# Hybrid decoder block on one core: a conv chunk goes first, vector steps follow a hand-written table, GpSimd makes four low halves

## What is computed

```
h = rms_norm(x);  proj = h @ w_in          # ca, cg, q, k, v, iq, ik, iw, z, xbc, dt
conv: u = ca * sigmoid(cg); u = causal depthwise conv of 31 taps
      u = silu(layer_norm(u))
att:  scores of 4 indexer heads -> top 128 keys of each query; softmax attention on them, 8 heads
ssm:  conv of 4 taps and silu on xbc; chunked state-space scan (4 chunks of 128); gate silu(z), rms_norm
x = x + concat([conv, att, ssm]) @ w_out
f = causal conv of 3 taps on rms_norm(x) @ w_up;  x = x + (silu(fg) * fa) @ w_down
```

## Time and profile before

| | us |
|---|---|
| median of 3 runs | 768.38 (765.89 to 770.06) |
| the profiled execution: its own time | 770.06 |
| its span, first to last instruction | 768.3 |
| slot 0 begins | 19.2 |
| slot 12 begins | 69.96 |
| slot 64 begins | 277.56 |
| slot 76 begins | 333.73 |
| the FFN begins | 403.4 |

### The profile page before, as it was taken

How to read it: one execution, slowest core, us unless ns; L and a number is a source line. 1 busy time by engine, 2 the same in 40 slices (tenths; PEclk the granted TensorE clock), 3 DMA queues, 4 the chain that set the end, 5 groups by cost and what they waited for, 6 DMA issues and landing times.

```text
span 768.3 us, 9446 instructions
## 1 busy us (share of the span) xinstructions
PE 729.4 (95%) x3430; PEld 580.7 (76%) x3430; DVE 476.2 (62%) x731; ACT 331.5 (43%) x498; POOL 98.9 (13%) x79
## 2 busy tenths in 40 slices
PE   3999988799999989999969999999999999999998
PEld 2767876676666668888848888888888888888886
DVE  5357899977999957666673656565656665212222
ACT  6245464678546664722443344434443434110110
POOL 2000576642000003333020000000000000000000
PEclk9999999999999999999988999999999999999999
DMA  8541312311111142032221323333243322333302
GB/s 263 150 153 56 110 55 56 110 56 56 55 55 55 56 165 93 23 106 55 82 55 55 110 72 91 109 109 87 77 109 109 98 72 103 110 109 110 104 6 110
DMA packets 78047, 69.46 MB, mean 90 GB/s; under 512 B 5815, under 2 KB 64535, under 8 KB 78015
## 3 DMA queue, kind: packets, MB, share of 16 engines
q1 hardware_dynamic: 77871, 68.51, 28.9%
q10 hardware_dynamic: 144, 0.52, 0.2%
HBM read 66.91 MB, written 2.12 MB: 90 GB/s over the span
## 4 chain that ended last, share of the span: by engine, by line
PE 71%; DVE 12%; ACT 6%; issue 5%; POOL 4%; DMA 1%; SPq 0%; DVEq 0%; POOLq 0%; ACTq 0%
PE bank L1442 62%; DVE u_acc L565 3%; POOL stats L724 2%; DVE w_lo L575 2%; POOL u_acc L744 2%; PE bank L1448 2%; PE bank L1462 2%; ACT w_hi L813 1%; DVE xbcT L1249 1%; DMA x_in<-in_x 1%; PE bank L1684 1%; PE bank L1658 1%; DVE prob L1228 1%; PE bank L1632 1%; ACT prob L928 1%
## 5 line engine op out<-in xcount | busy, mean ns | idle before, releaser
L1442 PE MATMUL bank<-h_hi,w_hi 128*128 128x512 f32 x480 | 192.1, 400 | 1.8 <-DVE h_lo L1080 1.8
L1442 PE MATMUL bank<-h_lo,w_hi 128*128 128x512 f32 x480 | 188.5, 393 | 0.0
L1442 PE MATMUL bank<-h_hi,w_lo 128*128 128x512 f32 x480 | 188.4, 393 | 0.0
L575 DVE TENSOR_TENSOR w_lo<-w_raw,w_hi 128x2048 fp32r<-128x2048 f32 x34 | 79.8, 2348 | 80.7 <-ACT w_hi L813 80.7
L1442 PEld LDWEIGHTS bank<-h_hi,w_hi 128*128 128x128 f32 x480 | 91.2, 190 | 29.3 <-issue 10.6
L1442 PEld LDWEIGHTS bank<-h_hi,w_lo 128*128 128x128 f32 x480 | 91.0, 190 | 19.7
L1442 PEld LDWEIGHTS bank<-h_lo,w_hi 128*128 128x128 f32 x480 | 91.3, 190 | 18.0
L1403 DVE SCALAR_TENSOR_TENSOR f<-bank,prm,f 128x511 f32<-128x511 f32 x88 | 65.8, 747 | 58.1 <-ACT f L1049 51.8
L813 ACT ACTIVATE w_hi<-w_raw 128x2048 fp32r<-128x2048 f32 x34 | 64.9, 1910 | 80.9 <-PE bank L1442 80.3
L1049 ACT ACTIVATE f<-bank,prm 128x512 f32<-128x512 f32 x44 | 33.8, 769 | 102.2 <-PE bank L1442 102.2
L1442 PE MATMUL bank<-w_hi,g_hi 128*128 128x512 f32 x176 | 68.5, 389 | 0.0
(11 more groups left out here) (225 smaller groups left out, 1022.7 us busy)
## 6 DMA issues: line engine op xcount, KB each, us to landing
w_raw<-in_w_up SPq DMA_DIRECT2D x44, 512.0 KB, 4.7
w_raw<-in_w_in SPq DMA_DIRECT2D x34, 512.0 KB, 4.7
w_raw<-in_w_down SPq DMA_DIRECT2D x22, 512.0 KB, 4.4
w_raw<-in_w_out SPq DMA_DIRECT2D x12, 512.0 KB, 4.2
x_in<-in_x SPq DMA_DIRECT2D x4, 512.0 KB, 6.7
tbias<-distance_table SPq DMA_DIRECT2D x1, 2048.0 KB, 8.2
x<-in_x SPq DMA_DIRECT2D x4, 512.0 KB, 6.5
out_x<-y_out SPq DMA_DIRECT2D x8, 256.0 KB, 2.0
```

The source lines that it names most:

```text
L575: eng.tensor_tensor(wlo[:, slot, cols], wraw[:, slot, cols], whi[:, slot, cols].bitcast(F32), ALU.subtract).then_inc(ready, 1)
L1442: ins = pe.matmul(o, a, b, start=first and i == 0 and q == 0, stop=last and i == n - 1 and q == 2)
```

## The change

The order of the plan changes, two step kinds change their ring, and four low halves change their engine. Conv 0 becomes the first chunk and the indexer's the second. `TOP_SLOTS` and `DW_SLOTS` go; the table `FILL` gives for each slot a string, each letter of which takes the next step of a stream: 1, 2, 3 are the top-k steps of a block (with its `sel` at the end), a, c, d are the taps of tiles 0, 2 and 3. Tile 1 is now POOL's, its taps spread from slot 15 to 60 (before: tile 0, 15 to 44). The scores of the indexer move from slots 5, 6, 8 to slots 8 to 11. `ln` moves from slots 66, 67 to 70, 71 and `lnT` from 70, 71 to 73, 74, all in the ring acc. The four `xt` steps stand in slots 65 and 66, two each, where all stood in 65. POOL makes the whole low half of chunks 6, 8, 9 and 10 (before: `POOL_LO` is empty, DVE makes all); who needs one of them waits for POOL's semaphore.

```diff
-CHUNKS = [("iq", 0), ("conv", 0), ("conv", 1)]
+CHUNKS = [("conv", 0), ("iq", 0), ("conv", 1)]
...
-TOP_SLOTS = {1: (9, 36), 2: (9, 42), 3: (9, 48)}
-DW_SLOTS = [(15, 44), (14, 50), (42, 63), (46, 65)]
-LN_SLOTS = (66, 66, 67, 67)
-LNT_SLOTS = (70, 70, 71, 71)
+FILL = {6: "aa", 7: "aaa", 8: "aaa", 10: "1121", 11: "1212", 12: "31213", 14: "2131", 
+        15: "21321", 16: "32112", 18: "31", 19: "23", 20: "121", 21: "3123", 22: "121a", 
+        23: "32131", 24: "2a1321", 25: "32", 26: "1a", 27: "23", 28: "112", 29: "3a1", 
+        30: "23121", 31: "a312", 32: "312a132", 33: "132a23", 34: "23a", 35: "232", 36: "a323", 
+        37: "2a32", 38: "32a33", 39: "a3a3", 40: "3a3a", 42: "cccc", 43: "cccca", 44: "ccac", 
+        46: "dddd", 47: "d", 48: "dddc", 50: "dca", 51: "d", 52: "cdca", 54: "dcd", 55: "c", 
+        56: "dacdd", 58: "cad", 59: "cd", 60: "cdac", 62: "dcda", 63: "cdcd", 64: "dcdc", 
+        65: "dc", 66: "dcdcd", 67: "cdd"}
+POOL_SLOTS = (15, 60)
+LN_SLOTS = (70, 70, 71, 71)
+LNT_SLOTS = (73, 73, 74, 74)
-DW_POOL = 0
+DW_POOL = 1
-POOL_COLS = 640
-POOL_LO = []
+POOL_LO = [6, 8, 9, 10]
...
-    put(3, ("ev", "iq", 0), ("ev", "iq", 1), ("small",), ("ev", "ik", 0))
+    put(3, ("ev", "cg", 0), ("ev", "ca", 0), ("small",), ("ev", "ik", 0))
-    for n, b in ((5, 1), (6, 2), (8, 3)):
-        put(n, *[("idx", b, h) for h in range(NIH)])
+    for n, b, hs in ((8, 1, (0, 1, 2, 3)), (9, 2, (0, 1, 2, 3)), (10, 3, (0, 1)), (11, 3, (2, 3))):
+        put(n, *[("idx", b, h) for h in hs])
...
-        fill[(n if j else at[("conv", 1)]) + 5].append(("glu", j))
+        fill[n + 5].append(("glu", j))
+    spread([("dw", DW_POOL, i) for i in range(CONV_K)], *POOL_SLOTS)
+    spread([("dwp", DW_POOL, i) for i in range(1, CONV_K)], POOL_SLOTS[0] - 1, POOL_SLOTS[1] - 1)
+    for n, letters in FILL.items():
+        fill[n] += [next(streams[v]) for v in letters]
     for t in range(NT):
-        put(LN_SLOTS[t], ("ln", t))
+        fill[LN_SLOTS[t]].append(("ln", t))
         front[LN_SLOTS[t] + 1].append(("lnn", t))
     for j in range(4):
-        put(LNT_SLOTS[j], ("lnT", j))
+        fill[LNT_SLOTS[j]].append(("lnT", j))
-    put(s0 + 1, *[("xt", t) for t in range(NT)])
+    for t in range(NT):
+        put(s0 + 1 + t // 2, ("xt", t))
...
+        elif k in ("ln", "lnT"):
+            group(*s)
...
+        def low(eng, c, ready):
+            eng.wait_ge(w_hi_ready, c + 1)
+            slot = c % NSLOT
+            eng.tensor_tensor(wlo[:, slot, :], wraw[:, slot, :], whi[:, slot, :].bitcast(F32),
+                              ALU.subtract).then_inc(ready, 1)
+        def dve_los(c):
+            return c + 1 - sum(p <= c for p in POOL_LO)
+        def wait_low(eng, c):
+            if c in POOL_LO:
+                eng.wait_ge(pool_lo_ready, POOL_LO.index(c) + 1)
+            else:
+                eng.wait_ge(w_lo_ready, dve_los(c))
```

More of the change, by code:

```diff
@@ L124, in make_plan @@
         fill[4 * c - 3].append(("lo", c))
+    streams = {str(b): iter([(k, b, r) for r in range(TOPK // 8) for k in ("topmax", "topmark")]
+                            + [("sel", b)]) for b in (1, 2, 3)}
+    for j in range(4):
+        streams["abcd"[j]] = iter([("dw", j, i) for i in range(CONV_K)])
     def spread(steps, a, b):
@@ L135, in make_plan @@
     put(2, ("prm",))
-    put(3, ("ev", "iq", 0), ("ev", "iq", 1), ("small",), ("ev", "ik", 0))
+    put(3, ("ev", "cg", 0), ("ev", "ca", 0), ("small",), ("ev", "ik", 0))
     put(4, ("iwT",), ("dt", 0))
-    put(6, ("dt", 1))
-    put(8, ("dt", 2))
-    for n, b in ((5, 1), (6, 2), (8, 3)):
-        put(n, *[("idx", b, h) for h in range(NIH)])
-    for b in (1, 2, 3):
-        spread([(k, b, r) for r in range(TOPK // 8) for k in ("topmax", "topmark")], *TOP_SLOTS[b])
-        fill[TOP_SLOTS[b][1]].append(("sel", b))
+    put(5, ("dt", 1))
+    put(6, ("ev", "iq", 0), ("dt", 2))
+    put(8, ("ev", "iq", 1))
+    for n, b, hs in ((8, 1, (0, 1, 2, 3)), (9, 2, (0, 1, 2, 3)), (10, 3, (0, 1)), (11, 3, (2, 3))):
+        put(n, *[("idx", b, h) for h in hs])
     put(1, ("gtab",))
@@ L175, in make_plan @@
         n = at[("conv", j)]
-        put(n + 2, ("ev", "cg", j))
-        put(n + 4, ("ev", "ca", j))
-        fill[(n if j else at[("conv", 1)]) + 5].append(("glu", j))
[L179 to L182, removed]
+        if j:
+            put(n + 2, ("ev", "cg", j))
+            put(n + 4, ("ev", "ca", j))
+        fill[n + 5].append(("glu", j))
[3 more added lines that the diff above has]
+        fill[n] += [next(streams[v]) for v in letters]
     for t in range(NT):
-        put(LN_SLOTS[t], ("ln", t))
+        fill[LN_SLOTS[t]].append(("ln", t))
         front[LN_SLOTS[t] + 1].append(("lnn", t))
     for j in range(4):
-        put(LNT_SLOTS[j], ("lnT", j))
+        fill[LNT_SLOTS[j]].append(("lnT", j))
     for m in range(8):
@@ L251, in make_groups @@
         k = s[0]
-        if k in ("prm", "idx", "ln", "lnT", "qkT", "cs", "iwT", "yT"):
+        if k in ("prm", "idx", "qkT", "cs", "iwT", "yT"):
             aux.append(s)
+        elif k in ("ln", "lnT"):
+            group(*s)
         elif k == "score":
@@ L746, in _ @@
                 elif k == "lo" and s[1] in POOL_LO:
-                    part_lo(pool, s[1], pool_lo_ready)
+                    low(pool, s[1], pool_lo_ready)
                 elif k == "seg":
@@ L1145, in _ @@
                         op1=ALU.mult).then_inc(dta_ready, 1)
-                elif k == "lo":
-                    part_lo(dve, s[1], w_lo_ready)
+                elif k == "lo" and s[1] not in POOL_LO:
+                    low(dve, s[1], w_lo_ready)
                 elif k == "glu":
@@ L1424, in _ @@
             for c in range(DN0 + 1, len(CHUNKS)):
-                part_lo(dve, c, w_lo_ready)
+                low(dve, c, w_lo_ready)
             for t in range(NT):
@@ L1523, in _ @@
                             pe.wait_ge(hi_evac, HIGH.index(("hT", NT - 1, 1)) + 1)
+                            claim(pe, "cg", 0)
+                            claim(pe, "ca", 0)
                             first_pass(whi, hhi, True, False)
@@ L1740, in _ @@
                 c = DN0 + j
[L1741 removed]
+                wait_low(pe, c)
                 pe.wait_ge(glo_ready, 2 * j + 3)
```

28 lines of the change are left out of this document (8 added, 20 removed).

## The result

The changed kernel takes **779.15 us** (median, 777.46 to 780.66) against 768.34 for the kernel before on the same chip: ratio 1.0145 [1.0114, 1.0177], slower by 10.8 us. The forecast was 766.7 with a range of 758 to 776, so the result lies outside it, on the side of rival (c). The profiled execution took 777.46 us, its span is 775.7 (before 768.3). One execution of a later version (the split of `xt` alone) took 1463 us with every matmul of 512 columns at 677 ns; it is left out of that version's comparison by time, and the version ran once more for a profile.

The account below looks back on a forecast made before the run. PE, busy 95% of the span, was taken as the bound, with DVE pacing it in the middle stages. Terms -0.5 - 5.1 + 0 - 4.5 + 6.7 + 1.7 = -1.7 us against the median 768.38 gave 766.7, range 758 to 776.

Parts of the forecast that it names:

- rival (c): Slower: waits at slots 71, 74, 76 each bring a clock drop, low halves stop DVE 4.1 us; about 776; 0.30 with (d).
- its own lateness is hidden: POOL's low halves: done 5 us after the high half ends, while PE needs them 11 us after the slot began.
- The price of a lock: DVE stopped by each POOL low half: 2.5 us taken, bounds 0.6 and 4.1, top-k steps covering part.
- the strict rule: DVE and GpSimd's shared pair is locked for the whole instruction, so each POOL low half costs DVE 4.1 us.
- slots 12 to 35: DVE relieved but still setting the pace at 76.9 us against PE's 69.9; counted as -5.1 us.
- The late layer norm: Slots 70 to 76: new PE waits of +3.0, +3.2 and +4.8 us at slots 71, 74 and 76, sum +11.0.
- they lie close together, so I take one: Slots 70 to 76: three stalls of 3 to 5 us counted as one clock drop, +1.7 us, ends 0 and +5.
- 47 to 63: Slots where DVE loses 14 of 41 taps and PE becomes the bound: -4.5 us of 5.1 to win.
- 64 to 69: Slots where splitting xt covers ACT's copy: -2.4, clock drop -1.7, start -0.2, sum -4.3 us; -5.9 with moved transposes.
- Rival (a): POOL's low halves stop DVE under 1 us each, first stage PE-bound: total -10.7 us, 757.7; chance 0.26.
- (b): Late layer norm hidden, DVE entering slot 70 with less behind it: half of 11.0 goes, -7.2, about 761; chance 0.10.
- (d): ACT, behind POOL in its scaling steps, holds attention's exps in slots 38 to 58: 771; counted into the slower case, 0.30.

Follow-up runs that it names:

- the first version: The kernel before with only the late layer norm (ln in slots 70 and 71, lnT in 73 and 74, both in the ring acc): 785.45 us, ratio 1.0257.

## Why the prediction was wrong

**Where it failed first: "its own lateness is hidden."** The forecast had the high half end 3 us into slot 4c - 4 and POOL done 5 us later. In the trace ACT's high half of chunk 8 ended at 128.33, 9.6 us into its slot, because ACT stood for POOL's taps (and POOL, before that, for DVE's sums of squares), and POOL then did a power and a tap first. PE waited 7.9 us at chunks 6 and 8. Put right by itself the lateness gave back 3.4 us up to the logit, but only 0.9 at slot 47, since the locks stayed. I had read ACT's waits for POOL's taps and used them against the scalings only, not against the `hi` step behind them in the same queue. The operation was mis-sized too: 4.8 us in the middle, 4.1 forecast.

**The price of a lock.** The value taken was 2.5 us per low half, between 0.6 and 4.1. Measured: 3.6, 4.0 and 3.8, and next to nothing for the fourth. The choice rested on top-k steps standing in between; but POOL started while DVE was just ahead of a norm step or a mask, and only 0.9, 0.8 and 0.2 us of the three lengths were covered by steps that ran on. Three low halves stand ahead of the logit, so this is 3.9 us more of DVE's time. For these three the upper end was right, and the strict rule with it; the fourth had the cover that was hoped for. With the low halves back on DVE the same stretch takes 78.8 us, where the forecast's own sum without locks is 63.9 + 6.9 + 5.5 = 76.3: the count of DVE's work was off by 2.5 us, the two terms for POOL by more: together they were to cost 0.6 us net (7.5 for locks less 6.9 of work), and cost 6.4. Of the 9.6 us between the forecast and the profile 8.0 lie in this stage and 4.9 in the layer norm's. Instead of -5.1 the slots 12 to 35 gave +2.9.

**The late layer norm.** The three waits were forecast at 3.0, 3.2 and 4.8 and came at 3.2, 3.5 and 5.2: mechanism and sizes right, and the run with this part alone shows them again. What failed is the term behind them: "they lie close together, so I take one" drop, 1.7 us. The stretch grew by 19.2 us; less 1.6 of moved transposes and 11.9 of waits, some 5.7 are left, with a granted clock of 0.91 to slot 76 and slot 76 itself at 1.2 GHz for the most part. The end kept for it, +5, was nearly right. The size of 1.7 a drop was read from stages said to have "a stall of over 2 us"; in the one from 199.9 to 262.8 the longest is 1.97 us, and before the change a stall of 2.16 us at 133.90 had no drop behind it, so the rows did not carry a rule of one drop for one long stall.

**What held.** Slots 0 to 11 (-1.0 for -0.5), 47 to 63 (-5.2 for -4.5, with PE as the bound and the drop gone), and 64 to 69 (-6.0 for -5.9). But the last one was put down to the split of `xt` alone, and that is wrong: alone it costs 2.5 to 4 us, and it needs the layer norm out of slot 66, so that this number came out was partly luck. Slots 36 to 46 gave 2.0 us where 0 was forecast; the 2.5 us kept there for the fourth lock did not come.

**The rivals.** Rival (c) said: each wait its drop, and the locks at full length, about 776. That is what happened but for the fourth lock, and with the lateness, which no rival had, it became 779.15. Rival (a) is excluded by the locks' lengths, (b) by the waits, which the first version shows unchanged in the old plan. Of (d) ACT's waits for POOL were real, but held the high half, not the exps.

**Where the 10.8 us come from**, by the medians: the layer norm's ring and place +14.0, POOL's low halves +5.3 (+4.2 beside the other), the split -4.2, and the rest, the new first chunks, the table, tile 1 in place of tile 0 on POOL and the late slots of the layer norm, -4.3, which no run takes apart: the version without POOL's low halves, with the old ring and the old `xt`, is 764.05 against 768.34 (and against 767.5 in its own comparison, -3.5). With each version set against the kernel before as measured beside it, the terms are +13.1, +5.4, -4.2 and -3.5, with the same sum.

## What to carry to other kernels

When a step is given to another engine, follow the queues that feed it, not only its own: it starts when the last step ahead of it on the producer's queue and on its own is done, and the producer can already be waiting for the engine that gets the work. And of two causes that overlap, taking one away may win nothing: here neither shorter locks nor an earlier start brought a gain by itself. In these runs work moved from DVE to GpSimd cost time where DVE paced PE and had a step beside it that was held, 2.3 us of relief against up to 4.0 us of standing, and brought nothing where PE was the bound. And a wait that is removed must be checked for what it covered: the same two-slot split gave 4.2 us in one plan and cost 2.5 to 4 in the other.

## What the runs showed that was not expected

- A DVE step with a single SBUF input is held as well: the mask, 128 x 256 from float32 to bfloat16, took 4.59 us beside a POOL low half, and a `TENSOR_SCALAR` of 128 x 8 took 2.82. The top-k steps beside POOL, which have one SBUF input too, kept their lengths.
- The length of a single PE wait does not tell whether a drop of the clock follows. Waits of 2.43, 5.51 and 5.22 us had matmuls of 0.63 us behind them (at 104.30, 135.24 and 339.49), the one of 3.35 us at 154.15 had none; the wait for the logit in the same place before the change, 3.17 us, had a granted clock of 0.50 from 153 to 156 us. Waits of 1.7, 0.6 and 0.6 us in slots 73 and 74 left the clock at 1.00 in one version and came with 0.50 in another. In the layer norm's stretch the slower clock cost about half as much as the waits themselves.
- The same low half on POOL took 4.57 to 4.59 us in the later chunks and 4.6 to 5.0 in the middle, where DVE works beside it; cut in four at the same place, 6.4.
